# A two-block transformer on one core: own tiles of the first norms ahead of the others, gate rows one per weight tile, products that wait tile by tile

## The reference

```python
# first block, layers L0 and L1 (xl: 256 own tokens, xc: 256 context tokens)
mod = silu(c) @ w_mod[l] + b_mod[l]            # six rows of 1024: shift, scale, gate, twice; modc from c_ctx
h  = rms_norm(xl, g_pre_mix[l]) * (1 + sc1) + sh1       # hc the same of xc
# q, k, v of h (k, v also of hc), rope, differential attention; conv branch; pooling branch
m  = sigmoid(h @ w_g + b)[a,b,c] * (y_a, y_b, y_c), summed;   y = m @ w_out
xl = xl + gt1 * rms_norm(y, g_post_mix[l])
h  = rms_norm(xl, g_pre_ffn[l]) * (1 + sc2) + sh2
xl = xl + gt2 * rms_norm((silu(h @ wa) * (h @ wb)) @ w_ffn_out[l], g_post_ffn[l])
# xc is updated in the same way in L0 only
# second block, layers E0 and E1 (own x, 256 memory tokens mem)
proj = rms_norm(x, norm_mix) @ w_in
# E0: index scores choose 64 keys per query, attention over them; E1: three dilated attentions
mo = attention(q_m, rms_norm(mem, norm_mem) @ w_mem_kv)
x = x + concat(mix, mo) @ w_out
x = x + swiglu(rms_norm(x, norm_ffn))
# at the end rms_norm(x, final_norm)
```

## Time and profile before

| | us |
|---|---|
| median of 3 runs (2500.51 to 2506.31) | 2504.98 |
| the profiled execution | 2509.98 |
| its span | 2508.2 |

### The profile page before, as it was taken

One profiled execution on the slowest core, in us unless ns is written; L12 is line 12 of the kernel. 1 busy time (PEld: TensorE's weight loads), 2 busy tenths in 40 slices (PEclk: granted clock), 3 DMA queues, 4 the chain that ended last, 5 costly groups with the idle time before them and its releaser, 6 DMA issues. The chain is left out here.

```text
span 2508.2 us, 32933 instructions
## 1 busy us (share of the span) xinstructions
PE 2286.0 (91%) x13160; PEld 1896.3 (76%) x13160; DVE 1376.0 (55%) x2091; ACT 883.9 (35%) x1410; POOL 196.4 (8%) x242
## 2 busy tenths in 40 slices
PE   3999988999979999996998898899799899898998
PEld 1667745887757777785885788898687799797997
DVE  2377577545353333225956766665574565565664
ACT  2222265223232222223324544444343434444443
POOL 2082100000010000002420000000100000000000
PEclk8899999999989999997999999899795899899999
DMA  7344225332224444223431455465550566452664
GB/s 243 114 118 147 97 70 153 90 106 77 91 69 118 134 135 142 84 93 93 136 104 40 126 163 173 136 188 192 143 135 1 150 186 197 130 172 65 183 189 133
DMA packets 428660, 320.81 MB, mean 128 GB/s; under 512 B 25811, under 2 KB 379725, under 8 KB 428509
## 3 DMA queue, kind: packets, MB, share of 16 engines
q1 hardware_dynamic: 426108, 310.77, 41.7%
q0 software_dynamic: 2368, 7.93, 1.1%
q10 hardware_dynamic: 32, 0.01, 0.0%
HBM read 317.62 MB, written 1.05 MB: 127 GB/s over the span
## 5 line engine op out<-in xcount | busy, mean ns | idle before, releaser
L288 DVE TENSOR_TENSOR split<-raw,split 128x1024 fp32r<-128x1024 f32 x506 | 605.3, 1201 | 747.3 <-ACT split L285 746.3
L299 PE MATMUL PS<-HH,split 128*128 128x256 f32 (+1 forms) x2504 | 820.5, 328 | 42.1 <-DVE HL L293 20.3
L300 PE MATMUL PS<-HL,split 128*128 128x256 f32 (+1 forms) x2504 | 806.9, 322 | 0.0
L301 PE MATMUL PS<-HH,split 128*128 128x256 f32 (+1 forms) x2504 | 805.7, 322 | 0.0
L285 ACT ACTIVATE split<-raw 128x1024 fp32r<-128x1024 f32 x506 | 513.6, 1027 | 545.8 <-PE PS L301 467.6
L299 PEld LDWEIGHTS PS<-HH,split 128*128 128x128 f32 x2504 | 481.4, 192 | 97.4 <-DVE HL L293 21.9
L301 PEld LDWEIGHTS PS<-HH,split 128*128 128x128 f32 x2504 | 480.8, 192 | 39.0
L300 PEld LDWEIGHTS PS<-HL,split 128*128 128x128 f32 x2504 | 481.4, 192 | 36.8
L299 PE MATMUL PS<-split,UH 128*128 128x512 f32 x440 | 174.7, 397 | 0.0
L300 PE MATMUL PS<-split,UH 128*128 128x512 f32 x440 | 173.9, 395 | 0.0
L301 PE MATMUL PS<-split,UL 128*128 128x512 f32 x440 | 173.9, 395 | 0.0
(11 more groups left out here) (244 smaller groups left out, 2606.9 us busy)
## 6 DMA issues: line engine op xcount, KB each, us to landing
raw<-in_w_in_dram SPq DMA_DIRECT2D x120, 512.0 KB, 4.1
raw<-in_w_ffn_in_dram SPq DMA_DIRECT2D x88, 512.0 KB, 4.1
raw<-in_l_w_gate_up_dram SPq DMA_DIRECT2D x88, 512.0 KB, 3.9
G<-in_w_mod_dram SPq DMA_DIRECT2D x86, 512.0 KB, 3.9
raw<-in_w_ffn_out_dram SPq DMA_DIRECT2D x44, 512.0 KB, 3.5
raw<-in_l_w_down_dram SPq DMA_DIRECT2D x44, 512.0 KB, 4.4
raw<-in_l_w_in_dram SPq DMA_DIRECT2D x30, 512.0 KB, 4.1
raw<-in_w_attn_out_dram SPq DMA_DIRECT2D x16, 512.0 KB, 4.1
```

The lines of the kernel that those rows point to most:

```text
L288: eng.tensor_tensor(c["low"], c["raw"], c["high"].bitcast(F32), ALU.subtract).then_inc(low_done, 1)
L299: pe.matmul(out, a[0], b[0], start=first, stop=False)
L300: pe.matmul(out, a[0], b[1], start=False, stop=False)
L301: return pe.matmul(out, a[1], b[0], start=False, stop=last)
```

## The change

Nothing is computed otherwise except that O2L is subtracted from PSUM. What moves:

- `norm_act`, `norm_dve`, `norm2_act`, `norm2_dve`, `norm_pe`, `rstd_pool` take a range `lo` to `hi` of tiles. L0 runs all four as before. L1 runs tiles 0 and 1, then the first projection; TensorE transposes tile 2 after the first chunk's product and tile 3 after the second's. E0 and E1 do the same with the memory tiles. ScalarE in L1 waits for all eight parts before its first sigmoid.
- L1: GpSimd forms the 1/rms of tiles 0 and 1 first, then clears only the halos of UP and PP (four memsets), then tiles 2 and 3, then the two DMAs.
- Start: ScalarE and VectorE hold all splits until the mod rows of L0's norm are out.
- Gates: one part per weight tile. For gt1 TensorE makes part p after the ya product of tile p + 2, for gt2 after the down product's chunks 0, 1, 5, 6; the results go to bank 7.
- y of the first block waits for `merged` k + 1 ahead of k tile k, y of the second block for the group k // 4 of the transposes, which now run group by group.
- In the second block ScalarE writes O2H straight from PSUM and VectorE subtracts from PSUM.

```diff
-    def norm_dve(dve, name, src, tiles, hf, scale, bias, ready):
+    def norm_dve(dve, name, src, tiles, hf, scale, bias, ready, lo=0, hi=None):
...
+        for n in range(lo, hi):
+            t = tiles[n]
             ready(dve, t)
+            if n >= 2:
+                wait_result(dve, (name, tiles[n - 2], 1))
             dve.wait_ge(S(name + "_rstd"), n + 1)
...
-            if n >= 1:
+            if n > lo:
                 parts(n - 1, tiles[n - 1])
+        parts(hi - 1, tiles[hi - 1])
...
+    def gate_pe(T, pe, l, part, p):
+        keys = gate_parts(l, part)
+        if not 0 <= p < len(keys):
+            return
+        key = keys[p]
+        gate_count[0] += 4
+        pe.wait_ge(S("diagonals"), gate_count[0])
+        ps = T.open(("gate",) + key, (BANKS - 1,))
+        T.close(pe.matmul(ps, ones[:, :], diagonal[:, key[3], :], start=True, stop=True), ("gate",) + key)
...
-        then()
-        product(T, pe, L + "ffn", w_down, FT, D, tiles, lefts(U), before=lambda k: pe.wait_ge(S(L + "hidden"), k + 1), last=last)
+        product(T, pe, L + "ffn", w_down, FT, D, tiles, lefts(U), before=lambda k: pe.wait_ge(S(L + "hidden"), k + 1), fill=down, last=last)
...
# TensorE, first block
-            norm_pe(T, pe, L + "n1", [0, 1, 2, 3])
-            norm_wait(pe, L + "n1", [0, 1, 2, 3])
+            first = 4 if n == 2 * SEQ else 2
+            norm_pe(T, pe, L + "n1", [0, 1, 2, 3], 0, first)
+            norm_wait(pe, L + "n1", [0, 1, 2, 3][0:first])
...
                     mod_pe(T, pe, L + "proj", 2 * j + (nm == "glu"))
+                    if j == 0 and first == 2:
+                        k = 2 + (nm == "glu")
+                        norm_pe(T, pe, L + "n1", [0, 1, 2, 3], k, k + 1)
...
+                    if number == 1:
+                        gate_pe(T, pe, l, 0, j - 2)
...
-            pe.wait_ge(S(L + "merged"), KT)
-            product(T, pe, L + "y", A["w_out"][l], KT, D, tiles, lefts((MTH, MTL)))
+            product(T, pe, L + "y", A["w_out"][l], KT, D, tiles, lefts((MTH, MTL)), before=lambda k: pe.wait_ge(S(L + "merged"), k + 1))
...
+                   lambda c: gate_pe(T, pe, l, 1, c if c < 2 else c - 3 if c > 4 else -1))
# ScalarE, first block
+        now["hold"] = True
         for q in range(KT * len(phases["start"])):
             mod_act(act, "start", q)
...
-        keep_splitting(act, ("turn",) + phases["start"][-1])
...
+            norm_wait(act, L + "n1", [0, 1, 2, 3])
             for j in range(NCH):
                 key = (L + "glu_gate", j)
...
-                if nm == "ya":
-                    gates_act(act, l, 0)
+                    if nm == "ya":
+                        gate_act(act, l, 0, j - 3)
...
# GpSimd, first block, layer L1
-                pool.memset(UP[:], 0.0).then_inc(S("filled"), 1)
-                pool.memset(PP[:], 0.0).then_inc(S("filled"), 1)
+                rstd_pool(pool, L + "n1", [0, 1, 2, 3], D, "_rstd", 0, 2)
+                for halo in (UP[:, :, :, 0:HALF_W], UP[:, :, :, HALF_W + SEQ:], PP[:, :, :, 0:POOL_PAD], PP[:, :, :, POOL_PAD + SEQ:]):
+                    pool.memset(halo, 0.0).then_inc(S("filled"), 1)
+                rstd_pool(pool, L + "n1", [0, 1, 2, 3], D, "_rstd", 2, 4)
# VectorE, first block
+        now["hold"] = True
         wait_read(dve, ("cols", 2, 0))
         wait_read(dve, ("cols", 0, 0))
         for group in phases["start"]:
             mod_columns(dve, group)
+        now["hold"] = False
         wait_read(dve, ("cols", 1, 0))
...
-            gates_dve(dve, l, 1)
+            for p in range(4):
+                if p == 2 and len(tiles) > 2:
+                    split_until(dve, (L + "ffn_up", FT - 1), AHEAD + 2)
+                gate_dve(dve, l, 1, p)
# second block
-            norm_pe(T, pe, L + "n1", [0, 1, 2, 3])
-            norm2_wait(pe, L + "n1", [0, 1, 2, 3])
+            norm_pe(T, pe, L + "n1", [0, 1, 2, 3], 0, 2)
+            norm2_wait(pe, L + "n1", [0, 1])
...
+            def memory_norm(j):
+                if nm == PROJ[e][0][0] and j < 2:
+                    norm_pe(T, pe, L + "n1", [0, 1, 2, 3], 2 + j, 3 + j)
...
-            pe.wait_ge(S(L + "ot_parts"), 2 * (OUT_TILES[e] // 4))
-            product(T, pe, L + "y", pname(e, "w_out"), OUT_TILES[e], D, [0, 1], lefts((O2H, O2L)), last=2)
+            for g in range(OUT_TILES[e] // 4):
+                out_transposes(g)
+            product(T, pe, L + "y", pname(e, "w_out"), OUT_TILES[e], D, [0, 1], lefts((O2H, O2L)), last=2,
+                    before=lambda k: [wait_read(pe, (L + "ot", t, k // 4)) for t in range(2)])
...
-                    read_out(act.activation(HF2[:, n % 2, :], bank(key), ACT.Copy), key)
+                    act.activation(O2H[to], bank(key).rearrange("p (k c) -> p k c", k=4), ACT.Copy).then_inc(S(L + "ot_high"), 1)
...
-                    split_value(dve, O2H[to], O2L[to], HF2[:, n % 2, :].rearrange("p (k c) -> p k c", k=4)).then_inc(S(L + "ot_parts"), 1)
+                    read_out(dve.tensor_tensor(O2L[to], bank(key).rearrange("p (k c) -> p k c", k=4), O2H[to].bitcast(F32), ALU.subtract), key)
```

More of the change, by code:

```diff
@@ L398, in columns, with rstd_pool @@
         read_out(ins, key)
-    def rstd_pool(pool, name, tiles, width, sem):
+    def rstd_pool(pool, name, tiles, width, sem, lo=0, hi=None):
         c = norm_cols(name)
-        for n, t in enumerate(tiles):
+        for n in range(lo, len(tiles) if hi is None else hi):
             pool.wait_ge(S(name + "_squares"), n + 1)
@@ L476, in norm2_wait, with norm_pe @@
                 wait_read(pe, (name, t, g))
-    def norm_pe(T, pe, name, tiles):
-        for n, t in enumerate(tiles):
+    def norm_pe(T, pe, name, tiles, lo=0, hi=None):
+        for n in range(lo, len(tiles) if hi is None else hi):
             pe.wait_ge(S(name + "_xn"), n + 1)
-            transposes(T, pe, name, t, XN[:, n % 2, :])
+            transposes(T, pe, name, tiles[n], XN[:, n % 2, :])
     def transposes(T, pe, name, t, src):
@@ L710, in gate_parts, with gate_dve @@
         return [(l, part, m, h) for m in range(layer_tokens(l)[0]) for h in range(2)]
-    def gates_dve(dve, l, part):
+    def gate_dve(dve, l, part, p):
+        keys = gate_parts(l, part)
+        if p >= len(keys):
+            return
         dve.wait_ge(S("gates"), 2 * l + part + 1)
[L714 to L734, removed]
+        _, _, m, h = keys[p]
@@ new lines, in gate_dve @@
+        if m:
+            wait_result(dve, ("gate", l, part, m - 1, h))
+        for k in range(4):
+            kt = 4 * h + k
+            dve.tensor_scalar(diagonal[:, h, k * P:(k + 1) * P], ident[:, :], mod[:, l, GATE_2 if part else GATE_1, kt, m:m + 1],
+                              None, ALU.mult).then_inc(S("diagonals"), 1)
+    def gate_pe(T, pe, l, part, p):
+        keys = gate_parts(l, part)
+        if not 0 <= p < len(keys):
+            return
+        key = keys[p]
[3 more added lines that the diff above has]
+        T.close(pe.matmul(ps, ones[:, :], diagonal[:, key[3], :], start=True, stop=True), ("gate",) + key)
@@ L736, in build, with gate_act @@
+    def gate_act(act, l, part, p):
+        keys = gate_parts(l, part)
+        if not 0 <= p < len(keys):
+            return
+        key = keys[p]
+        wait_result(act, ("gate",) + key)
+        _, _, m, h = key
+        read_out(act.activation(G[:, m, h * 512:(h + 1) * 512], bank(("gate",) + key), ACT.Copy), ("gate",) + key)
     gate_count = [0]
@@ L740, in build, with ffn_pe @@
     units_of = {l: [(t, h) for t in layer_tokens(l)[2] for h in range(HEADS)] for l in range(DEPTH)}
-    def ffn_pe(T, pe, L, w_up, w_down, tiles, n, U, wait, fill=nothing, then=nothing, last=1):
+    def ffn_pe(T, pe, L, w_up, w_down, tiles, n, U, wait, fill=nothing, down=nothing, last=1):
         norm_pe(T, pe, L + "n2", tiles)
```

112 lines of the change are left out of this document (59 added, 53 removed).

## The result

| | before | changed |
|---|---|---|
| median, us | 2505.64 (4 runs, 2500.51 to 2509.75) | 2467.11 (4 runs, 2458.64 to 2468.15) |
| profiled execution | 2509.98 | 2467.89 |
| its span | 2508.2 | 2466.1 |

The ratio is 0.9839 with a 95% interval of 0.982 to 0.9858: 38.5 us less by the medians, 42.1 less between the two profiled executions. The prediction said 2469, in 2456 to 2484.

A forecast was written before the change was run, and what follows sets the result against it. TensorE, busy 91% of the span, was taken as the bound, so its idle and half-clock stretches counted. Terms summed to -36.1 us from the profiled 2509.98, giving 2473.9; less 5.0 for the median, 2469 us, range 2456 to 2484.

The forecast's parts named there:

- Start: L0's first norm: with splits held back, the first XN comes at 48.5 instead of 51.32; -2.8 us.
- Gate parts: gt1 and gt2 made between products, without waits: -3.9 and -5.1 us in L0, -2.3 and -2.3 in L1.
- The slower rival: ScalarE's waits for gate results starve the splits at all twelve parts: 2547 us; chance 0.05.
- Products y: First block's y: gaps of 2.70 (L0) and 1.77 (L1) go, each with 1.7 of clock fall; -4.4 and -3.4 us.
- The clock doesn't come back: Rival: clock falls remain at both y products and come at two gate parts, 6.8 us, giving 2475.8; chance 0.10.
- n1 of L1: L1's first norm: first product 12.6 earlier, less transposes 2.2, a split wait 2.5 and clock fall 1.7; -6.2 us.
- The page weighed there: Skill page against the L1 term: GpSimd's 1/rms contends with VectorE's X update, first XN and median up to 0.9 us later.
- n1 of E0: E0's first norm: first product 6.5 earlier, but later angles, transposes and a clock fall outweigh it; +1.1 us.
- +4.8, +1.1 and +1.7: Costs in E0's norm term: a later split behind the angles, one set of transposes, and a clock fall.
- n1 of E1: E1's first norm, no angles: first product 6.3 earlier, transposes cost 2.2; -4.1 us.
- Transposes of O2 in E0: E0's y product starts with group 0 instead of waiting for the last low part; -2.1 us.
- The rest: Everything outside the priced steps, including halo memsets and ScalarE's norm wait in L0; put at nothing.

The follow-up runs named there:

- x9_hold: Changed kernel with VectorE's wait for the second column set moved inside the hold at the start; 2464.45 us, ratio to before 0.9829.
- x1_gates: Changed kernel with the gate parts again made in one go, no split issued ahead; 2481.71 us, ratio to before 0.9927.
- x2_y: Changed kernel with the first block's y products again waiting for all eight merged tiles; 2475.08 us, ratio to before 0.9891.
- x6_e0four: Changed kernel with all four tiles of n1 ahead of the first projection in E0 only; 2465.0 us, ratio to before 0.9848.
- x7_angles: Changed kernel with E0's rope angles ahead of the memory tiles' norm, those tiles transposed after the qm products; 2466.9 us, ratio to before 0.9825.
- x8_ot: Changed kernel with the second group of E0's output transposes in PSUM banks 0 and 1 instead of 4 and 5; 2463.68 us, ratio to before 0.9834.

## Why the prediction was right

The number came closer than its sum. Between the profiled executions -36.1 was forecast and -42.1 measured, 6.0 apart. The run before that was profiled lay 4.3 us above its median and the changed kernel's 0.8, which takes 3.6 of it back, and the 5.0 that I subtracted instead of 4.3 takes another 0.7. That part is luck. Term by term:

**Start.** Right in mechanism: XN stood behind splits 0 and 1, which the wait behind the hold still issues. It came at 47.59, not 48.5. x9_hold shows that these splits held it: without them it stands at 42.78 and waits for GpSimd's 1/rms.

**Gate parts.** All four terms within 0.5 us, by the same subtraction: idle and group away, 0.9 a part back. In L1 the wait ahead of yb stayed, at 2.37 us, and took 1.5 us of half clock with it, the 1.7 of that term. x1_gates gave back each of the four. The slower rival, ScalarE's waits for gate results, would have shown as waits for splits beside the parts, and the full size of the gains leaves no room for it.

**Products y.** The sum was right for the two traces and nearly half of it, 3.4 of 7.8, for a wrong reason. The gaps of 2.70 and 1.77 went, as said. The 1.7 us at half clock that I put behind each was there before and not after, but x2_y has both gaps without it. That part came true by luck. "The clock doesn't come back" asked the wrong question as well: a gap of this size doesn't decide whether the clock falls.

**n1 of L1.** Right in size (-6.2, measured -6.5, and 2.3 less again in the second profile of the same kernel), and the wait of 2.5 us came as 2.37. The first product moved by 12.1 (12.6 said), the two sets of transposes took 1.5 (2.2 said). But the step said "a wait on a split", and it was a wait on a PSUM bank: ScalarE's first sigmoid stood behind `norm_wait`, with its result tile unread. I had ScalarE's wait in the text and costed it only through the splits behind it, so the size was right by luck. Before the change all 8 transposed groups were read before the first product. Now 4 of them stand among the first gate and branch tiles in one rotation of seven banks, so the eighth opening met the first gate tile, still unread.

*The page weighed there.* GpSimd's 1/rms beside the last X update took 1.45 us, against 0.54 alone, and VectorE waited 0.50 for it ahead of XN. The Trainium skill (GPSIMD Engine Reference, "Specifications") says that the two share their interfaces to SBUF and contend where VectorE reads two inputs from it. The trace agrees, at about half of the 0.9 us that I named as its most:

```profile
1130.63 1.45 POOL L412 TENSOR_TENSOR rstd<-ms,half 128x1 f32<-128x1 f32 x1
```

**n1 of E0.** The first product came 6.4 earlier, as said (-6.5), and of +4.8, +1.1 and +1.7 behind it I see +3.2, +1.6 and +2.9. The sum holds, two terms were mis-sized against each other. There was already a wait of 1.78 at this place, in an earlier chunk, so the new 4.84 counts only partly. The clock's part was larger: 3.8 behind the wait, less 0.9 ahead of it. The angles began 3.4 us later against L1's last product, not 5.2. And what bounds the stage wasn't complete. The row on which I built, VectorE's first angle instruction at 1795.52, says in its brackets that it was released by a DMA after 2.64 us of idle. I used its start and passed over its releaser. That is why no order of VectorE's work alone helped (x6_e0four, x7_angles).

**n1 of E1.** -4.1 predicted, -6.6 measured. The first product moved by 6.1, much as said (6.3). Behind it the two sets of transposes took 1.6 back (2.2 said), and 2.1 came from the clock: before, TensorE was at 1.2 GHz until 2188.4, 5.3 us past its first product; in the changed kernel it was at 2.4 GHz from the first product on. By x2_y and the repeated profile this part isn't for certain the change's. No experiment undid the order in E1 alone.

**Transposes of O2 in E0.** The one term that came to nothing: -2.1 predicted, +0.3 measured. I wrote that a bank is free only after VectorE, and looked only at the transposes. Product y opens its first two results in the two banks of the transposes, and they are freed by the very last low part, so waiting group by group gave nothing. x8_ot puts the second group elsewhere and gains 2.6.

**The rest**, -3.8 us, is in stretches that the change doesn't touch; the repeated profile shows such shifts of up to 2.3 us a stage without any edit. It was put at nothing and came out in the change's favour by chance, as far as the runs show.

## What to carry to other kernels

Idle ahead of an instruction can be added up place by place, and the sum holds, if for each place one also asks what comes next in every queue: the next split, the next bank, the next DMA. Read the releaser of each row that carries a term, not its start alone. A wait per tile in place of a wait for all is worth nothing as long as the consumer opens a buffer that the last tile still holds. When own rows are moved ahead of others, much or all of the gain at the start may be given back within a few chunks (5.6 of 12.1 us, and 7.9 against 6.4, here).

## What the runs showed that was not expected

The granted clock of a stretch isn't fixed by the gap ahead of it. Behind a gap of 2.70 us it was 0.77 in one kernel and 1.00 in another; behind one of 2.37 (2.36) it was 0.76 and 1.00 in two executions of the same kernel. So a gap's price in clock can't be read from one profile. E0's attention, with 236 matmuls and no change in them, took 63.8 us at a mean of 0.50 in one kernel and 36.6 us at 0.95 in another. Less the 2.7 us of the banks that is 24.5 us in one stretch, against the 38.5 us of the whole change. Three kernels have runs in two groups, 20 to 24 us apart by their middle runs, so it seems that one kernel does either from run to run; no profile of both shows it.
